# A hybrid decoder step on one core: one instruction block, and the compressed chains of the samples one prompt unit earlier

## What is computed

```python
q, kcr, vcr, ks, vs, kw, vw, gates, z, gate = nsa_inputs(...)     # projection
kc, vc, c_end = compressed_kv(kcr, vcr, ...)                      # pool 32 rows, 2-layer MLP
p_c = masked_softmax(q . kc);  o_c = p_c . vc                     # branch 1, compressed
imp = p_c.sum(heads) . overlap;  top_idx = top_k(imp + forced)    # which 64-row blocks
o_s = softmax(q . k[top_idx]) . v[top_idx]                        # branch 2, selected
o_w = softmax(q . kw) . vw                                        # branch 3, window 512
y = (g0*o_c + g1*o_s + g2*o_w) * silu(z);  out = x + gate * (y . w_out)
```

## Time and profile before

| | |
|---|---|
| median of 3 runs | 1231.68 us (1231.11 to 1237.3) |
| profiled execution, its own time | 1234.1 us |
| span of the profiled execution | 1232.4 us |
| PE busy | 1163.0 us (94%) |
| mean granted clock of TensorE | 0.978 |
| HBM read | 227.57 MB |

### The profile page before, as it was taken

The page is one execution under the profiler, slowest core; times in us unless marked ns, Lnnn a source line. Parts: engine busy times, 40 slices in busy tenths (PEclk is TensorE's granted clock), DMA queues, the critical chain, the costliest instruction groups (busy, mean ns, idle before and its releaser), DMA issues. The chain is left out here.

```text
span 1232.4 us, 25152 instructions
## 1 busy us (share of the span) xinstructions
PE 1163.0 (94%) x9077; PEld 732.1 (59%) x9077; DVE 488.1 (40%) x1500; ACT 425.1 (34%) x1079; POOL 203.6 (17%) x345
## 2 busy tenths in 40 slices
PE   3899999999999999999998999999999599999995
PEld 1677774676767757477876555555555244544552
DVE  2444032344532421112203665656566323443445
ACT  3322112233321321010111565665656234444453
POOL 0000000000000102011102222222223524444300
PEclk9899999999999999999899999999999989999998
DMA  9654435303054302125004787667666999999972
GB/s 381 277 205 171 165 137 189 137 1 137 1 210 154 128 10 76 70 76 191 5 1 146 278 273 246 223 222 242 226 216 224 304 315 341 357 356 356 351 275 78
DMA packets 96551, 238.76 MB, mean 194 GB/s; under 512 B 12714, under 2 KB 50732, under 8 KB 91948
## 3 DMA queue, kind: packets, MB, share of 16 engines
q1 hardware_dynamic: 73036, 164.95, 38.1%
q0 software_dynamic: 23392, 72.21, 16.4%
HBM read 227.57 MB, written 17.05 MB: 198 GB/s over the span
## 5 line engine op out<-in xcount | busy, mean ns | idle before, releaser
L407 PE MATMUL ps<-arena,wring 128*128 128x288 f32 x1408 | 361.8, 414 | 2.0 <-ACT arena L547 2.0
L407 PEld LDWEIGHTS ps<-arena,wring 128*128 128x128 f32 x1408 | 266.8, 193 | 84.2 <-issue 12.3
L1721 POOL DMA_DIRECT2D arena<-in_cmp_pages x128 | 69.8, 546 | 269.8 <-PE ps L1886 100.0
L418 PE MATMUL ps<-wring,arena 128*128 128x512 f32 x192 | 90.1, 604 | 0.0
L1814 DVE CUSTOM_DVE_ANT_0 wring<-ps,wring 128x128 f32<-128x128 f32 (+3 forms) x128 | 57.6, 487 | 72.1 <-PE ps L1743 70.7
L2291 DVE CUSTOM_DVE_ANT_1 arena<-ps,small 128x512 f32<-128x512 f32 x64 | 44.2, 692 | 92.8 <-PE ps L2208 92.7
L1806 ACT ACTIVATE wring<-ps 128x128 f32<-128x128 f32 (+3 forms) x128 | 49.0, 436 | 86.6 <-PE ps L1766 86.6
L2267 ACT ACTIVATE arena<-arena 128x512 f32<-128x512 f32 (+1 forms) x88 | 57.0, 649 | 50.3 <-DVE arena L2307 50.3
L1792 ACT ACTIVATE wring<-wring 128x128 f32<-128x128 f32 (+3 forms) x128 | 70.7, 559 | 8.3 <-DVE wring L1814 8.3
L2278 ACT ACTIVATE arena<-ps 128x512 f32<-128x512 f32 x72 | 43.0, 597 | 81.7 <-PE ps L2229 81.7
L1879 PE MATMUL ps<-arena 128*32 128x256 f32 x1024 | 69.5, 389 | 0.4 <-DMA arena<-in_cmp_pages 0.4
(11 more groups left out here) (392 smaller groups left out, 1597.7 us busy)
## 6 DMA issues: line engine op xcount, KB each, us to landing
wring<-in_weights SPq DMA_DIRECT2D x27, 2048.0 KB, 10.1
arena<-in_cmp_pages POOLq DMA_DIRECT2D x128, 256.0 KB, 4.4
arena<-in_cmp_pages SPq DMA_DIRECT2D x128, 256.0 KB, 3.6
wring<-in_kv_pages SPq DMA_DIRECT2D x64, 256.0 KB, 11.3
wring<-in_kv_pages POOLq DMA_DIRECT2D x64, 256.0 KB, 7.1
arena<-in_kv_pages SPq DMA_DIRECT2D x50, 256.0 KB, 8.8
arena<-in_kv_pages POOLq DMA_DIRECT2D x50, 256.0 KB, 7.0
out_win_k_out<-in_win_kv SPq DMA_DIRECT2D x8, 512.0 KB, 12.1
```

The lines of the kernel that those rows point to most:

```text
L407: last = pe.matmul(out[:, 0:HT], w[:, k, ct * P:ct * P + P], moving[k][:, half * HT:half * HT + HT], start=(k == 0), stop=(k == KT - 1))
L418: last = pe.matmul(main, tokens, w[:, k, :], start=(k == 0), stop=(k == KT - 1))
L1721: eng.dma_start(cring[q % CR][:, 2 * half + j, :], v["cmp_pages"][bass.ds(ids[2 * d + j], 1)] .rearrange("o p c -> (o p) c")).then_inc(c_i ...
```

## The change

1. **One block.** The block boundary between projection and attention goes; each engine's lists are joined.
2. **Compressed chains one unit forward.** `pe_fill` is called with n = i // SU + 1: sample 0 is pooled between the last projection units (two groups after each of units 25 to 28), sample n+1 in unit n, and sample 7's chain is in unit 7. The ninth unit is gone; three bare steps remain. To have banks 0 and 1 for this, the last 8 projection units use two bank pairs instead of three. Sample 0's groups use two slots in turn, as the other two are the projection's input; `prompt_cmp_scores(0)` and its softmax move between the last two projection units.
3. **Sample 0.** Its keys alone go into the eight halves of the four compressed slots, as sample 7's groups 4 to 7 are pooled; 7 of its 10 scores are in unit 7 (banks 0 and 1), 3 in the bare steps. Its values come into the same homes, each after the score of that group. So they are 64 page loads of 128 KB instead of 32 of 256 KB. The prompt's last gate stands after sample 0's last scores on DVE.
4. **Homes from sample 1 on** are chosen anew, so that every values home lies above its keys home: one DMA each time. Sample 1's loads stand behind sample 0's last values in both queues.

```diff
+        late_sets = end_a + [chunk for chunk, _, _ in plan_c].index(W_ZC)
...
+            if u >= late_sets:
+                return 2 - (u - late_sets) % 2
...
+            return u - 1 if two_sets <= u < end_a or u >= late_sets else u - 2
...
+            def after_unit(i):
+                if i == len(plan_c) - 2:
+                    pe.wait_ge(act_p, AC2["vcs"])
+                    pe.wait_ge(dve_p, DV2["kcT"])
+                    prompt_cmp_scores(pe, 0)
+                prompt_compressed(i)
+                if len(plan_c) - 5 <= i < len(plan_c) - 1:
+                    for g in range(2):
+                        pe_pool(pe, 0, 2 * (i - len(plan_c) + 5) + g)
...
+        def page_slot(q):
+
+            return q % 2 if q < NG else q % CR
...
+                if q in (NG + 2, NG + 3):
+                    eng.wait_ge(proj_done, u0c + len(plan_c))
+                elif q >= 2:
+                    before = q - 2 if q < NG + 2 else q - CR
+                    eng.wait_ge(pe_c, PC_["pool", before // NG, before % NG])
...
+        k_homes = ring[0:4] + [vv0, vv1, c0, s0]
+        v_homes = [ring[5], ring[6], ring[7], ring[9], LAST_KEYS, z0, z1, c1] + [ring[8], ring[10], ring[11], ring[4], s1, s2, HEAD_KEYS, s3]
+        first_k, first_v = page_homes + [ring[4]], page_homes + [HEAD_KEYS]
...
+        def wait_keys_home(eng, n, i):
+
+            at = (n - 1) * NL + i
+            if n == 0 and i < NG:
+                eng.wait_ge(pe_c, PC_["pool", NB - 1, NG // 2 + i // 2])
+            elif n == 0:
+                eng.wait_ge(pe_a, PE3["t", 3 * SU, 0])
+            elif at < 4:
+                eng.wait_ge(pe_a, PE3["t", tile_step[at - 4], 1])
+            elif at < 6:
+                eng.wait_ge(pe_a, PE3["pv", U - 1])
             elif at < KR:
+                eng.wait_ge(valued, page_homes.index(k_homes[at]) + 1)
+            else:
+                eng.wait_ge(scored, ((at - KR) // NL + 1) * NJ + (at - KR) % NL + 1)
+
+        def wait_values_home(eng, n, i):
+
+            at = (n - 1) * NL + i
+            if n == 0 and i < NG:
+                eng.wait_ge(scored, i + 1)
...
+        def sp_third(sp):
+            for pair in range(NB * NG // 2):
+                load_cmp(sp, 0, pair)
+                if pair == 0:
+                    sp.wait_ge(proj_done, unit_end[W_ZC])
+                    sp.dma_start(pmask, v["prompt_masks"]).then_inc(in_pm, 16)
+            load_window_keys(sp, 0)
+            for pair in range(NG // 2):
+                load_keys(sp, 0, 0, pair)
+            sp.wait_ge(pe_c, PC_["turn", NB - 1, 1])
+            sp.dma_start(rows_all, v["out_tiles"][0]).then_inc(tile_in, 16)
+            for pair in range(NG // 2):
+                load_values(sp, 0, 0, pair)
+            for n in range(1, NB):
+                for pair in range(NG // 2):
+                    load_kv(sp, 0, n, pair)
+                load_window_keys(sp, n)
+                sp.wait_ge(tile_done, n)
+                sp.dma_start(rows_all, v["out_tiles"][n]).then_inc(tile_in, 16)
...
+        def pe_third(pe):
+            pe_rows_turn(pe, 0, 1)
+            prompt_cmp_scores(pe, 1)
+            for i in range(U + 3):
+                if i < U and is_tile[i]:
+                    prompt_scores(pe, i)
+                if values_first(i) and i < U + 3:
+                    prompt_values(pe, i - 3)
+                if i < U:
+                    pe_fill(pe, i // SU + 1, i % SU, "a")
+                if 1 <= i - (U - SU) <= INSIDE:
+                    pe_scores(pe, 0, i - (U - SU) - 1)
+                if 2 <= i < U + 2:
+                    prompt_turn(pe, i - 2)
+                if i < U:
+                    pe_fill(pe, i // SU + 1, i % SU, "b")
+                if 3 <= i < U + 3 and not values_first(i):
+                    prompt_values(pe, i - 3)
+                if i >= U:
+                    pe_scores(pe, 0, INSIDE + i - U)
+                if i < U:
+                    pe_fill(pe, i // SU + 1, i % SU, "c")
```

More of the change, by code:

```diff
@@ L1892, in pe_rows_turn @@
             pe.wait_ge(act_c, AC_["rows", n, half])
+            if n == 0:
+                pe.wait_ge(*((dve_c, DC_["pooled", 0, 0]) if half else (dve_a, DV3["ca0"])))
             if n:
@@ L2166, in bring @@
[L2166 to L2174 removed]
+            return v_homes[((n - 1) * NL + i) % KS] if n else first_v[i]
@@ new lines, in page_of, with load_keys @@
+        def page_of(page):
+            return v["kv_pages"][bass.ds(page, 1)].rearrange("o p c -> (o p) c")
+        def load_keys(eng, half, n, pair):
+            ids = page_ids(eng, 0, ((n * (NG // 2) + pair) * 2 + half) * GP)
+            for d in range(2):
+                i = 2 * pair + d
+                wait_keys_home(eng, n, i)
+                for j in range(2):
+                    lo = (2 * half + j) * KVW
+                    eng.dma_start(keys_home(n, i)[:, lo:lo + KVW], page_of(ids[2 * d + j])[:, 0:KVW])\
+                        .then_inc(k_in[half][keys_sem(n, i)], 16)
@@ new lines, in act_third, with cmp_exp @@
+        def act_third(act):
+            def cmp_exp(gp):
+                act.wait_ge(dve_a, DV3["cm%d" % gp])
+                act.activation(pc[:, gp], pc[:, gp], ACT.Exp).then_inc(act_a, AC3.one("cexp%d" % gp))
+            cmp_exp(0)
+            for i in range(U + 2):
+                if i < U:
+                    act_fill(act, i // SU + 1, i % SU, "first")
+                if 2 <= i < U + 2:
+                    prompt_turned(act, i - 2)
+                if i < U:
+                    act_fill(act, i // SU + 1, i % SU, "a")
+                if i < U and is_tile[i]:
+                    prompt_exp(act, i)
+                if i < U:
+                    act_fill(act, i // SU + 1, i % SU, "b")
+                if i == 5:
+                    cmp_exp(1)
+            for n in range(NB):
+                act_exp(act, n, 0)
+                for at in range(NJ):
+                    if at < LAST:
+                        act_exp(act, n, at + 1)
+                    act_turned(act, n, at)
+            act.wait_ge(f_summed, 1)
+            act.activation(f_std[:, 0:TP], ps[:, 0, :], ACT.Sqrt, scale=1.0 / D, bias=eps[:, 0:1]).then_inc(f_rooted, 1)
+            act.wait_ge(s_rows, 1)
+            for half in range(2):
+                rows = slice(half * NS, half * NS + NS)
+                last = act.activation(s_tok[rows, :], ps[rows, 2 + half, :], ACT.Copy)
+            last.then_inc(s_copied, 1)
+            act.wait_ge(s_summed, 1)
+            act.activation(f_std[:, TP:NT], ps[:, 4, 0:NS], ACT.Sqrt, scale=1.0 / D, bias=eps[:, 0:1]).then_inc(s_rooted, 1)
@@ L2467, in _ @@
[L2467 to L2472 removed]
+                add_parts = pe_first(pe)
+                pe_between(pe, add_parts)
+                pe_second(pe)
+                pe_third(pe)
```

573 lines of the change are left out of this document (284 added, 289 removed).

## The result

The changed kernel takes 1226.38 us (median of 7 runs, 1221.26 to 1229.64); the kernel before, on the same chip, 1235.49 us (7 runs, 1231.11 to 1240.76). The ratio is 0.9922 (95%: 0.9900 to 0.9945), a gain of 9 us where 15 were forecast. The profiled execution is the longest of its seven, 1229.64 us with a span of 1228.0, so its 4.4 us against the span of before say less than the medians do.

A forecast was written before the change was run, and what follows sets the result against it. The prediction took the kernel as PE-bound with an idle hole before sample 0's output tile. Its terms, 3.8 - 1.2 + 9.7 + 3.6 - 1.0 = 14.9 us, off 1231.68 gave 1217 us; range for 8 in 10: 1208 to 1227.

The forecast's parts named there:

- Start of the attention: Between projection and unit 0: 1.5 us idle left (0.5 to 5.3) instead of 5.3, a gain of 3.8.
- The eight units: Prompt units of the attention: 6.0 us idle against 4.8 before, a loss of 1.2; unit 7 some 4 us shorter.
- The hole: PE's idle time between the last prompt unit and tile 0: 5 us instead of 14.7 (3 to 10), gain 9.7.
- Clock: PE's slow clock spell around tile 0 goes: gain 3.6 us (0 to 6), with 1 us left for another spell.
- The samples: From tile 0 on, DMA supply and PE's demand for the last keys meet: 1 us of stall (0 to 8).
- DMA supply falls short: Rival, chance 0.15: in the samples, loads at 340 GB/s take 6.8 us more, giving 1223 to 1225 us.
- lead shortened: Reason given for the supply rival: sample 1's loads begin 8 us ahead of tile 0 instead of 20.
- nothing changes: Rival, chance 0.03: the gain before tile 0 comes back as DMA waits in the samples, 1228 to 1237 us.
- a load lands some 2 us late: Landing delay in the samples' DMA sum, which put the last keys in 192 us after tile 0.
- about 8 us ahead: Start of sample 1's loads before tile 0, behind sample 0's last values in both queues; about 20 us before the change.

The follow-up runs named there:

- e7: Changed kernel split again into two instruction blocks, the boundary behind the last projection unit and sample 0's pooling: 1229.93 us, 0.9964 of the kernel before.
- e11: The changed kernel itself, unaltered, measured a second time: 0.9928 of the kernel before.
- e6: Changed kernel with sample 1's loads held until sample 0's first value product is done: 1.0045 of the kernel before.
- e2: Changed kernel with output tiles 1 to 7 loaded from ACT's queue in place of SP's: 0.9918 of the kernel before.
- e3: Changed kernel with sample 1's first two groups loaded ahead of sample 0's last values, on SP and POOL: 0.9910 of the kernel before.
- e4: Changed kernel with the prompt's last gate done by DVE one step earlier, before sample 0's last score: 0.9914 of the kernel before.
- e5: Changed kernel with one page load per group and queue instead of two, from sample 1's group 4 and sample 2's group 3 on, output not the reference's: 1215.89 us.
- e9: Changed kernel with page loads of samples 1 to 7 in 2 KB pieces instead of 1 KB, same bytes, output not the reference's: 1218.03 us.
- e1: Changed kernel with partitions 64 to 127 left out of most page loads of samples 1 to 7, output not the reference's: 0.9983 of the kernel before.
- e12: Changed kernel with sample 1's first loads and the last gate earlier, plus eight paired key-value areas taking 2 KB pieces: 1223.22 us, 0.9911 of before.

## Why the prediction was right or wrong

The sign and the kind of gain were right, the size was 6 us too large. The time is inside the range, at its upper end. Of the 9.4 us between the forecast of 1217 and the 1226.4 measured, 3.8 are the base: seven runs of the kernel before gave 1235.5, not the 1231.7 from which the forecast was counted.

*Start of the attention:* 1.55 us idle (34.36 less 32.81), 1.5 forecast; no wait for pages between the projection units. Right. The block boundary was not priced by itself; e7, with a boundary at this place, is 3.5 to 5 us slower.

*The eight units:* units as before, with 0.63 us idle; unit 7 is 33.2 us long, 2.8 shorter (some 4 forecast), with 1.2 idle. Some 1 us better than the 6.0 forecast.

*The hole:* 4.1 us idle (10.48 less 6.38), 5 forecast, in the two waits that were named: 2.15 us for DVE's normalising, 1.95 for the gate behind the last scores. Right, in size and releaser.

*Clock:* one spell at 0.84 before tile 0, tile 0 at 7.1 us. Not foreseen were the spells behind the waits in the samples, 0.83 from 1000 to 1010 us. Up to tile 0 the forecast adds up to 3.8 - 1.2 + 9.7 + 1.8 - 1.0 = 13.1 us and 17.5 were won; 1.9 of the surplus of 4.4 are idle time, the rest is busy time.

*The samples:* here the prediction fell. It put 1 us of stall; there are 11.3, or 10.2 by e11. Against the forecast 196.4 us (198.2, less the 2.8 of clock in sample 0, plus 1.0) tile 0 to tile 7 takes 206.3, 9.9 us too much; 4.4 were gained above the forecast before tile 0. That leaves 5.5 us, about what the medians miss. Both of its own conditions for being wrong, waits above 3 us for loads and a clock under 1.00 in samples 0 and 1, are what the profile shows (7.1 us, and 0.83). The measured 1226.4 lies between two rivals: "DMA supply falls short" (1223 to 1225, given 0.15), which had "lead shortened" as a reason but priced a lower rate, where the rate is the 352 GB/s of the forecast; and "nothing changes" (1228 to 1237, given 0.03), which had the mechanism, the gain of the hole coming back as DMA waits.

The step that failed is "a load lands some 2 us late". The sum compared 68.7 MB over 352 GB/s with the time at which PE wants the last keys, as if only the end had to be met. It left out that, with full queues, a load is issued into a backlog: the tiles landed 13.8 and 16.1 us after their issue. The kernel before shows this already. From 955 to 1185 us its DMA view and its SP timeline have

```profile
arena<-in_out_tiles SPq DMA_DIRECT2D x7, 512.0 KB, 11.6
...
1004.46 0.42 SPq L2400 DMA_DIRECT2D arena<-in_out_tiles  x1
```

So its tiles took 11.6 us to land, and PE waited for them only 0.2 us in all, since they went out early: tile 1 was issued 13.5 us behind tile 0, in the changed kernel 18.9 us (19.4 in e11). Of the 27.9 us in which PE does the work between two tiles, that leaves 9.0 us for the landing. It took 13.8, and the first period is 4.8 us too long; in e11 it was 8.5 against 18.4, and 10.0 too long.

The lead was mis-sized too: "about 8 us ahead" was 3.6, and 2.2 in e11. By the slope of e6 (0.8 to 1.0) the missing 4.4 us alone are worth some 4 of the 10, an estimate; how the stall divides between lead and landing no run shows.

Since the loads run at PE's pace (357 GB/s at share 1.05, from 1100 to 1180 us), no lead is rebuilt while PE does not wait; PE waits until the loads are far enough ahead, once. The old kernel had built its lead inside the hole: in the last 36 us before tile 0 its DMA engines were 0.93 busy at 310 GB/s, those of the changed kernel 0.41 at 127 GB/s in unit 7 and 0.37 at 107 GB/s in the bare steps. So the hole did work that the sum did not see, and 10 of its 15 us came back. e6 gives the slope: 12.7 us less lead cost 10.3 us, or 11.4 cost 11.5 when compared with e11.

Whether the 1.5 us by which tile 7 to the end is longer in some profiles (44.8 against 43.3) has to do with the change stays open: changed variants show both.

## What to carry to other kernels

Before you fill a hole in the busiest engine, ask what the other queues do in it: here the DMA queues built the lead on which seven samples lived. Where supply and demand run at the same rate, a lead is not rebuilt for free. For the first loads that the engine needs, compare the time between issue and use with the time from issue to landing, and take the latter from a row in which the queues are full: here 11.6 us before the change, and 13.8 to 18.4 after it. In this kernel each edit that removed one wait only moved it (e2, e3, e4); fewer loads (e5) and a higher rate (e9) shortened the sum. An earlier release of homes was not tried.

## What the runs showed of the hardware

*Piece length.* At a full DMA share loads in pieces of 1 KB ran at 351 to 358 GB/s (e11, 980 to 1020 us), the same bytes in pieces of 2 KB at 383 to 389 (e9, 980 to 1040 us), some 9% more. The Trainium skill, "DMA: Bandwidth & Descriptors", "Specifications", has a limit of about 358 GB/s on HBM for one core; here e9 goes beyond it, so it is not what held the loads at 352.

*Half the partitions.* e1 and e5 moved the same 214 and 215 GB/s between 1100 and 1180 us, e1 with loads to partitions 0 to 63 at a DMA share of 0.95, e5 with fewer loads to all 128 at 0.65. The changed kernel, with whole loads, had 357 GB/s at 1.05. So a load to 64 partitions takes nearly as long as one to 128. The Trainium skill, "SBUF — State Buffer", "Door 1: The DMA port swizzle", states that partitions 0 to 63 reach only half of the 16 ports. The trace agrees in direction: for the same rate e1's share is 1.5 times that of e5, with windows and tiles still going to all 128 partitions.

*Landing times.* The loads of tiles, 0.5 MB each, took 13.4 us from issue to landing in the changed kernel's samples (median of seven on SP's queue), 13.8 to 18.4 us where PE waited for them, and 21.1 us once in e12. Issued from ACT, whose queue had no other loads in this stretch, the same tiles took 6.6 us (e2, at a DMA share of 1.04 as in the changed kernel), and on SP's queue at the lower share of e5 7.3 us. So the landing time goes with what stands in the same queue, and not only with how busy the DMA engines are.
